# Sums of squares over the partitions as a high and a low fp32r product, in an SSD and HGRN2 trunk on one core

## The reference

```python
# SSD, 8 groups of 4 heads x 64 = 256 channels each
y = y * jax.nn.silu(z)
y = _rmsnorm(y.reshape(bt, length, SSD_GROUPS, D_SSD // SSD_GROUPS), ssd_norm_w)
# HGRN2, 8 heads of 128 channels each
o = o_f + o_b[:, ::-1]
o = _rmsnorm(o, hgrn_norm_w) * jax.nn.silu(hg)
```

## Time and profile before

| | us |
|---|---|
| median of 3 runs | 3067.2 (3065.01 to 3068.65) |
| the profiled execution's own time | 3067.05 |
| its span, first to last instruction | 3065.1 |
| TensorE busy (matmuls) | 3010.3, 98% of the span |
| weight loads | 2889.8, 94% |
| DVE, ACT, POOL busy | 1711.7, 1331.3, 939.6 |
| mean granted TensorE clock | 0.996 |

### The profile page before, as it was taken

The page is one execution under the profiler, slowest core; times in us unless marked ns, Lnnn a source line. Parts: engine busy times, 40 slices in busy tenths (PEclk is TensorE's granted clock), DMA queues, the critical chain, the costliest instruction groups (busy, mean ns, idle before and its releaser), DMA issues. The chain is left out here.

```text
span 3065.1 us, 61797 instructions
## 1 busy us (share of the span) xinstructions
PE 3010.3 (98%) x22660; PEld 2889.8 (94%) x22660; DVE 1711.7 (56%) x2959; ACT 1331.3 (43%) x2583; POOL 939.6 (31%) x1091
## 2 busy tenths in 40 slices
PE   7999999999999999999999999999999999999999
PEld 5899999999999999999999999999989999999999
DVE  4646757567467575674675533444267454545543
ACT  6445455455454554554545542212243222225432
POOL 0024445245244452452444510000213343430100
PEclk9999999999999999999999999999999999999999
DMA  7722122122221221221312234432312223236554
GB/s 268 249 83 91 41 81 82 43 77 87 64 93 41 78 85 41 78 87 59 98 41 77 87 125 143 137 116 85 108 44 59 75 68 82 64 94 215 174 168 122
DMA packets 339185, 299.83 MB, mean 98 GB/s; under 512 B 13192, under 2 KB 308208, under 8 KB 338928
## 3 DMA queue, kind: packets, MB, share of 16 engines
q1 hardware_dynamic: 293856, 229.45, 24.6%
q10 hardware_dynamic: 45072, 67.00, 6.9%
HBM read 246.95 MB, written 49.45 MB: 97 GB/s over the span
## 5 line engine op out<-in xcount | busy, mean ns | idle before, releaser
L858 PE MATMUL bank<-h_hi,w_hi 128*128 128x384 f32 x2496 | 867.9, 348 | 2.1 <-ACT th L1451 2.1
L858 PE MATMUL bank<-h_hi,w_lo 128*128 128x384 f32 x2496 | 835.8, 335 | 0.0
L858 PE MATMUL bank<-h_lo,w_hi 128*128 128x384 f32 x2496 | 835.1, 335 | 0.0
L858 PEld LDWEIGHTS bank<-h_hi,w_hi 128*128 128x128 f32 x2496 | 468.8, 188 | 17.2 <-issue 7.3
L858 PEld LDWEIGHTS bank<-h_lo,w_hi 128*128 128x128 f32 x2496 | 469.4, 188 | 2.7
L858 PEld LDWEIGHTS bank<-h_hi,w_lo 128*128 128x128 f32 x2496 | 468.5, 188 | 0.0
L1970 POOL TENSOR_TENSOR kq<-kq,fg 128x384 f32<-128x384 f32 x288 | 290.1, 1036 | 176.0 <-PE bank L987 145.0
L1516 DVE SCALAR_TENSOR_TENSOR acc<-bank,taps,acc 128x372 f32<-128x372 f32 (+5 forms) x512 | 249.2, 507 | 70.3 <-ACT acc L1150 59.2
L1238 ACT ACTIVATE cumb<-cumb,tok_g 128x128 f32<-128x128 f32 x576 | 176.6, 389 | 92.7 <-POOL cumb L1931 54.9
L2345 PE MATMUL bank<-a_hi,v_hi 128*128 128x384 f32 x480 | 163.3, 340 | 11.2 <-DVE v_lo L2791 5.1
L2345 PE MATMUL bank<-a_lo,v_hi 128*128 128x384 f32 x480 | 161.1, 336 | 0.0
(11 more groups left out here) (364 smaller groups left out, 6804.4 us busy)
## 6 DMA issues: line engine op xcount, KB each, us to landing
raw<-in_w_in SPq DMA_DIRECT2D x104, 512.0 KB, 4.1
raw<-in_ffn_w SPq DMA_DIRECT2D x96, 512.0 KB, 4.7
cumb<-cum_scratch SPq DMA_DIRECT2D x72, 512.0 KB, 6.0
ada_late<-in_ada_w SPq DMA_DIRECT2D x8, 2048.0 KB, 9.3
small<-gate_scratch ACTq DMA_DIRECT2D x72, 192.0 KB, 2.4
hid_scratch<-small SPq DMA_DIRECT2D x20, 576.0 KB, 3.6
gate_scratch<-th ACTq DMA_DIRECT2D x48, 192.0 KB, 1.9
y_scratch<-x_t SPq DMA_DIRECT2D x8, 1152.0 KB, 4.8
```

Source lines behind the costliest of these rows:

```text
L858: last = pe.matmul(out, w[i][:, k, :], h[:, k, blk(hb)], start=(k == 0 and j == 0), stop=(k == KT - 1 and j == 2))
```

## The change

The matrix of ones leaves the constants that are loaded and becomes an fp32r tile of its own, set by a memset in the setup; its fp32 view serves the remaining plain products. The sums of squares of SSD blocks 0 and 1 and of all three HGRN2 blocks are split in a high and a low fp32r part, and each sum is two fp32r products that accumulate in one bank. SSD block 2 stays a plain product. The semaphores of `mixers` are now drawn from the pool that is used again later. Diff, with parts that only allocate left out:

```diff
-K_ID, K_ONE = 0, 128
-K_EPS, K_EPS4, K_1, K_PICK, K_W = 256, 257, 258, 260, 292
+K_ID = 0
+K_EPS, K_EPS4, K_1, K_PICK, K_W = 128, 129, 130, 132, 164
...
+        ones_r = sb("ones_r", [P, P], F32R)
+        ident, ones = cst[:, K_ID:K_ID + P], ones_r[:, :].bitcast(F32)
...
-                mixers(nc, scope, sb, sem, locals())
+                mixers(nc, scope, sb, early_sem, locals())
...
         def _(dve):
             ch = Chain(dve_s)
+            dve.memset(m["ones"], 1.0)
...
+    sq_high, sq_split, osq_split = Count(sem("sq_high"), 2), Count(sem("sq_split"), 2), Count(sem("osq_split"), NB)
```

TensorE, `ssd` and `hgrn`:

```diff
-                if k >= SLOTS - NB:
-                    b = k - (SLOTS - NB)
+                for b in {SLOTS - 2: (0,), SLOTS - 1: (1, 2)}.get(k, ()):
                     bank = (S[3], S[4], S[0])[b]
-                    pe.wait_ge(sq_summed.sem, sq_summed.at(g, b + 1))
-                    pe.matmul(bank[:, 0:BW], ones, squares(b)[:, 0, :], start=True, stop=True).then_inc(ms_ready.sem, 1)
+                    if b < 2:
+                        pe.wait_ge(sq_split.sem, sq_split.at(g, b + 1))
+                        for e in (1, 0):
+                            last = pe.matmul(bank[:, 0:BW], ones_r[:, :], squares_split(b)[:, e, :],
+                                             start=(e == 1), stop=(e == 0))
+                        last.then_inc(ms_ready.sem, 1)
+                    else:
+                        pe.wait_ge(sq_summed.sem, sq_summed.at(g, b + 1))
+                        pe.matmul(bank[:, 0:BW], ones, squares(b)[:, 0, :], start=True,
+                                  stop=True).then_inc(ms_ready.sem, 1)
...
                 if k == O_SLOT + 1:
                     for n, b in enumerate(O_ORDER):
-                        pe.wait_ge(o_kept.sem, o_kept.at(g, n + 1))
-                        pe.matmul(S[b][:, 0:BW], ones, ktok[b], start=True,
+                        pe.wait_ge(osq_split.sem, osq_split.at(g, n + 1))
+                        pe.matmul(S[b][:, 0:BW], ones_r[:, :], kt_r[:, blk(b)], start=True, stop=False)
+                        pe.matmul(S[b][:, 0:BW], ones_r[:, :], at_r[:, blk(b)], start=False,
                                   stop=True).then_inc(hms_ready.sem, 1)
```

ACT, `ssd` (ahead of slot 16's evacuation) and `hgrn`:

```diff
+                if k == SLOTS - 2:
+                    for b in range(2):
+                        wait(sq_summed, g, b + 1)
+                        act.activation(squares_split(b)[:, 1, :], squares(b)[:, 0, :], ACT.Copy).then_inc(sq_high.sem, 1)
...
-                        act.activation(ktok[b], S[3 + b][:, 0:BW], ACT.Square).then_inc(o_kept.sem, 1)
+                        act.activation(at[b], S[3 + b][:, 0:BW], ACT.Square)
+                        act.activation(kt_r[:, blk(b)], S[3 + b][:, 0:BW], ACT.Square).then_inc(o_kept.sem, 1)
```

DVE, `ssd` (slot 16, after the update of `x_t`, ahead of `decay`), the new function, and its place in the loop's stage B; in the last group's stage B it is called right after `join_decays`, ahead of `low`:

```diff
+                if k == SLOTS - 2:
+                    for b in range(2):
+                        wait(sq_high, g, b + 1)
+                        dve.tensor_tensor(squares_split(b)[:, 0, :], squares(b)[:, 0, :],
+                                          squares_split(b)[:, 1, :].bitcast(F32), ALU.subtract).then_inc(sq_split.sem, 1)
...
+            def split_squares(g):
+                for n, b in enumerate(O_ORDER):
+                    wait(o_kept, g, n + 1)
+                    dve.tensor_tensor(at_r[:, blk(b)], at[b], kt_r[:, blk(b)].bitcast(F32),
+                                      ALU.subtract).then_inc(osq_split.sem, 1)
...
                     b_evac(g, k)
                     if k in JOINS and k > 4:
                         join_decays(g, k)
+                    if k == O_SLOT + 1:
+                        split_squares(g)
                     if k == SLOTS - 1:
                         hgrn_norm(g)
```

More of the change, by code:

```diff
@@ L172, in build @@
         hid_dram = nc.dram_tensor("hid_scratch", [HID, P, T], F32, kind="Internal").ap()
-        ident, ones = cst[:, K_ID:K_ID + P], cst[:, K_ONE:K_ONE + P]
+        ones_r = sb("ones_r", [P, P], F32R)
+        ident, ones = cst[:, K_ID:K_ID + P], ones_r[:, :].bitcast(F32)
         def x_rows(c):
@@ L535, in mixers @@
     cst, masks, vec, raw, banks, mod, cs = m["cst"], m["masks"], m["vec"], m["raw"], m["banks"], m["mod"], m["cs"]
-    ident, ones = m["ident"], m["ones"]
+    ident, ones, ones_r = m["ident"], m["ones"], m["ones_r"]
     h_hi, h_lo, w_src = m["h_hi"], m["h_lo"], m["w_src"]
@@ L589, in mixers @@
         y_tok = t_off[:, 0:GW]
+        with ExitStack() as later:
+            mm_r = sb("mm_r", [P, 2, 512], F32R, later)
+            cumb_r = sb("cumb_r", [P, 3, 8 * P], F32R, later)
         mm = sb("mm", [P, 2, 512], F32, ssd_scope)
@@ L598, in squares, with squares_split @@
             "p (e n) -> p e n", n=BW)
+    def squares_split(b):
+        if b == 0:
+            return mm_r[:, :, 0:BW]
+        return cumb_r[:, :, :].rearrange("p a n -> p (a n)")[:, T + (b - 1) * 2 * BW:T + b * 2 * BW].rearrange(
+            "p (e n) -> p e n", n=BW)
     with ExitStack() as hgrn_scope:
+        with ExitStack() as later:
+            kt_r = sb("kt_r", [P, 4 * BW], F32R, later)
         kt_all = sb("kt_all", [P, 4 * BW], F32, hgrn_scope)
@@ L607, in mixers @@
         hs_b = sb("hs_b", [P, NC - 1, P], F32, hgrn_scope)
+        with ExitStack() as later:
+            at_r = sb("at_r", [P, T], F32R, later)
         at_all = sb("at_all", [P, T], F32, hgrn_scope)
@@ L3257, in constants @@
     cst[:, K_ID:K_ID + P] = np.eye(P)
-    cst[:, K_ONE:K_ONE + P] = 1
     apart = (i[:, None] % BS) ^ np.arange(BS)[None, :]
```

## The result

| | before | after |
|---|---|---|
| median | 3066.45 (6 runs beside the kernel after; 3067.2 in the first three) | 3079.73 (6 runs, 3075.31 to 3080.67) |
| ratio, with its 95% interval | | 1.0039 [1.0029, 1.0049] |
| the profiled execution's own time | 3067.05 | 3079.28 |
| its span | 3065.1 | 3077.5 |
| mean granted TensorE clock | 0.996 | 0.994 |

The change makes the kernel slower by 13.3 us. The forecast was +8.5, with the right sign; the measured time lies in the range, near its upper end. Three of the four terms of the sum are in the profile close to what was forecast. Two things are missing from the sum: falls of the clock beyond the three assumed, and a term that it did not have at all.

What follows compares the result with a forecast made beforehand. The prediction took TensorE, busy 98% of the span, as the bound. From 3067.05, -4.2 (SSD) -0.9 (last group) +9.1 (waits) +4.5 (clock) = +8.5 us gave 3075.6, as a median 3075.7; range 3069 to 3081.

Steps and rivals of the forecast that it cites:

- The products, and SSD: Two fp32r products, 0.35 us, replace one of 0.65; SSD blocks 0 and 1 save 0.52 a group, -4.2 in eight.
- The chain to stage B: ACT's copies delay work leading to DVE's evacuation in stage B, which has 0.8 us of air; priced at nothing.
- Rival 3: ACT's chain to the SSD root loses its 0.8 us of air, stage B starts waiting: +12.7, 3079.9; chance 0.05.
- The last group: HGRN2's last group, outside the loop: three products save 0.30 us each without a wait, -0.9 us.
- The wait of the seven groups: HGRN2 in the loop: TensorE waits for splits behind DVE's evacuation of unit 16; 1.30 us a group, +9.1 in seven.
- Rival 4: HGRN2's splits are done before unit 16 is, so every pair saves 0.30: -11.4 us, 3055.8; chance 0.06.
- The clock: TensorE's stops of about 1.7 us in seven groups drop its clock, 1.5 us a fall; three falls taken, +4.5.
- Rival 1: The clock keeps its level or falls once at most: +4.0 to +5.5, 3071.2 to 3072.7; chance 0.32.
- Small parts, at nothing: Memset on DVE, smaller constants, POOL's few more semaphore clears and repeated use of semaphores; all priced at nothing.
- rival 2: The clock falls in five groups or more: +11.5 to +14.5, 3078.7 to 3081.7; chance 0.09.

Runs made afterwards that it cites:

- e1: Changed kernel with DVE's HGRN2 splits ahead of the evacuation of unit 16 in the loop, not behind it; 3057.97 us, 0.9970 of the kernel before.
- e6: Changed kernel with TensorE's three HGRN2 pairs one slot later, behind unit 17, DVE's stream as changed; 3060.72 us, 0.9976 of the kernel before.
- e8: e1 with HGRN2's three subtractions made in one and one wait for both SSD copies; 3054.76 us, 0.9957 of the kernel before.
- e5: Changed kernel with nine unread TensorE products filling the stop ahead of the wait for the first split; 3072.61 us, 1.0017 of the kernel before.
- e9: Changed kernel, unchanged, profiled once more to count falls of the clock; own time 3079.21 us.
- e10: Changed kernel, unchanged, profiled another time to count falls of the clock; own time 3080.13 us.
- e4: Changed kernel with neither split, only the fp32r ones with memset, smaller constants and reused semaphores; 3067.22 us, 1.0001 of the kernel before.
- e2: Changed kernel with the SSD part undone, HGRN2 part only; 3080.04 us, 1.0047 of the kernel before.
- e3: Changed kernel with the HGRN2 part undone, SSD part only; 3060.24 us, 0.9979 of the kernel before.

## Why the prediction was right and where it was wrong

- **The products, and SSD.** Right. Forecast -0.52 for a group, measured -0.57, which is nearly the bound of 0.58 that the prediction kept. The chain to stage B kept its 0.8 us of air. Rival 3 did not occur.
- **The last group.** Right: -0.9 forecast, -0.89 measured.
- **The wait of the seven groups.** Right to the hundredth: 1.30 us each, 9.1 in all. e1 and e6 show its cause by removing it from either side. Rival 4 (faster, 3055.8) is what e1 makes of the kernel: 3058.0, and 3054.8 in e8.
- **The clock.** The mechanism was right, and e5 shows it: same waits, no idle stop, no falls. The size of one fall was right (1.5 forecast; 1.57 in after, 1.45 to 1.60 in e9 and e10). Their number was under-sized. Three were taken; three profiles show two, four and four, and e5's 7.1 us agree with four to five. This term is nearer +6.3 than +4.5 in a usual execution. Rival 1, that the clock keeps its level or falls once at most, fits none of the three profiles. The Trainium skill (TensorE: Matmul & The Clock Gate, section Why this matters for your kernels) warns only of gaps clearly longer than these and would have had it so; the measurement decides against it for stops of 1.7 us.
- **"Small parts, at nothing".** This is the step that failed. e4 shows that the parts named there do cost nothing. But the list ended there: each instruction added to DVE was priced by its engine time alone, and the length of its loop body was not on it. Five more operations for a turn (two for SSD, three for HGRN2) brought one more instruction packet at each turn and lengthened DVE's restart behind its branch from 4.6 to 5.0 us to 5.4 to 6.3; TensorE then waited for `t_off`, and six turns cost 2.6 to 3.6 us. The trace of before had the warning: DVE idled for 4.2 to 4.5 us at each turn for "issue", and its first operation stood only 1.5 to 2.0 us ahead of TensorE.

With four falls and the turn as in e9 and e10 (2.6 to 2.9) the sum is -4.6 - 0.9 + 9.1 + 6.3 + 2.6 to 2.9 = +12.5 to +12.8, against a measured +13.3 between the medians.

That the range held the measured time is in part luck. At 3079.73 it lies in the band of rival 2 (3078.7 to 3081.7) and 0.2 us from the time of rival 3 (3079.9), and neither happened: at most four falls stand behind the stops, and stage B starts without a wait. The range went up to 3081 for their sake, and a term that the sum did not have filled that room.

What stays open: the sixth instruction packet at each turn comes with the long turn in every kernel here (100 to 102 packets in all with the short turn, 107 or 108 with the long one), and ten fillers bring both. That DVE starts late because it waits for this packet is inferred. The number of packets is not all of it: one turn of e4 restarted after 5.92 us with five. Where between three and five added operations the step lies was not tried. Nor is it known what decides in which groups the clock falls.

## What to carry to other kernels

Before you put work on an engine with idle time, look at what its stream does right ahead of that place: work behind an instruction that waits for the bottleneck cannot be ready when the bottleneck asks, however early its data are. Here the place of three instructions made 21.8 us, the falls of the clock included, where all the replaced products together were worth 11.9 (eight times 0.57, seven times 0.92, and 0.89). In a hardware loop count the instructions added to each body too, and see how far ahead of the bottleneck each engine restarts behind its branch.

## What the runs showed of the hardware that was not expected

- A loop body of DVE that grew by five or ten instructions restarted 5.2 to 6.3 us after its branch, with six instruction packets at each turn. Before, and with growth by two or three (e2, e3, e8), it was 4.6 to 5.3 us with five packets.
- A stop of TensorE of 1.7 us, followed by short bursts, was followed by a stretch at 1.2 GHz in ten of the 21 stops of the three profiles of the kernel after, at 1.45 to 1.60 us each. Nine products that nobody reads, run during the stop (e5), kept the clock up behind all seven stops of the profile, and the median was 7.1 us lower.
